# Five weight buffers with two filled early, a gather for each expert, and a later start of the first layer's modulation

## What is computed

```python
for l in range(DEPTH):                                   # first block, two layers
    proj = rms_norm(x, norm_g[l]) @ w_in[l]
    mixed = three_attentions(proj)
    x = x + mixed @ w_out[l]
mod = silu(c) @ w_ada + b_ada                            # 6 rows, and 2 for the end
x = x + gt1 * (attention(modulate(rms_norm(x), sh1, sc1)) @ w_out_2)
t = modulate(rms_norm(x, g_ffn), sh2, sc2)
g_idx = argmax(t @ w_rg + b_rg)                          # one of 4 groups
top_v, top_i = top_k(expert logits of that group, 2)     # two of its 8 experts
combine = softmax(top_v) * p_g, placed at the two experts
for e in range(32):
    a = silu(t @ w_gate[e]) * (t @ w_up[e])              # 2048 x 512, twice
    y = y + combine[:, e:e+1] * (a @ w_down[e])          # 512 x 2048
x = x + gt2 * y
return modulate(rms_norm(x, g_final), shf, scf)
```

## Time and profile before

| | |
|---|---|
| median of 3 runs | 2290.01 us (2289.23 to 2295.55) |
| the profiled execution | 2292.39 us, span of the trace 2290.6 us |
| PE busy | 2131.1 us, 93% of the span |
| PE weight loads busy | 1624.5 us, 71% |
| DVE busy | 1378.4 us, 60% |
| ACT busy | 727.2 us, 32% |
| moved by DMA | 761.71 MB, 333 GB/s over the span |

### The profile page before, as it was taken

The page is one execution under the profiler, slowest core; times in us unless marked ns, Lnnn a source line. Parts: engine busy times, 40 slices in busy tenths (PEclk is TensorE's granted clock), DMA queues, the critical chain, the costliest instruction groups (busy, mean ns, idle before and its releaser), DMA issues. The chain is left out here.

```text
span 2290.6 us, 35420 instructions
## 1 busy us (share of the span) xinstructions
PE 2131.1 (93%) x14355; PEld 1624.5 (71%) x14355; DVE 1378.4 (60%) x2159; ACT 727.2 (32%) x1317; POOL 40.8 (2%) x64
## 2 busy tenths in 40 slices
PE   7999999999999999899999979998888888888886
PEld 6799999888999998788997755554444444444443
DVE  6888899988888999755556453333333333333334
ACT  5444555454445554556555220000000000000001
POOL 0010000000000000120000000000000000000000
PEclk9999999999999999999999989999999999999998
DMA  9988777988887779654444199999999999999996
GB/s 345 353 334 320 290 276 278 356 340 344 321 324 280 282 282 373 233 213 148 138 150 163 37 385 430 430 430 430 430 430 430 430 430 430 430 430 430 430 430 282
DMA packets 72673, 761.71 MB, mean 333 GB/s; under 512 B 8256, under 2 KB 11248, under 8 KB 13936
## 3 DMA queue, kind: packets, MB, share of 16 engines
q1 hardware_dynamic: 72416, 759.37, 82.7%
q10 hardware_dynamic: 144, 0.79, 0.1%
HBM read 757.17 MB, written 2.96 MB: 332 GB/s over the span
## 5 line engine op out<-in xcount | busy, mean ns | idle before, releaser
L1218 DVE TENSOR_TENSOR s_w_tail<-s_raw,s_w_head 128x1024 fp32r<-128x1024 f32 x292 | 345.5, 1225 | 21.4 <-ACT s_w_head L827 20.9
L827 ACT ACTIVATE s_w_head<-s_raw 128x1024 fp32r<-128x1024 f32 x292 | 294.7, 1052 | 151.6 <-DMA s_raw<-in_w 97.2
L1006 PE MATMUL b_ps<-s_h_head,s_w_head 128*128 128x256 f32 x1184 | 341.8, 289 | 0.0
L1008 PE MATMUL b_ps<-s_h_head,s_w_tail 128*128 128x256 f32 x1184 | 334.8, 283 | 0.0
L1007 PE MATMUL b_ps<-s_h_tail,s_w_head 128*128 128x256 f32 x1184 | 334.8, 283 | 0.0
L1329 DVE CUSTOM_DVE_ANT_0 s_raw<-s_raw,s_c_row 128x2048 f32<-128x2048 f32 x128 | 292.5, 2285 | 3.6 <-DMA s_c_row<-c_row_dram 3.5
L2447 PE MATMUL b_ps<-s_raw,s_window 128*64 128x256 f32 x2048 | 227.6, 380 | 38.6 <-DMA s_raw<-in_w_up 20.6
L2447 PEld LDWEIGHTS b_ps<-s_raw,s_window 128*64 128x64 f32 x2048 | 155.1, 137 | 116.3 <-issue 30.6
L1006 PEld LDWEIGHTS b_ps<-s_h_head,s_w_head 128*128 128x128 f32 x1184 | 226.8, 192 | 1.9 <-issue 1.4
L1007 PEld LDWEIGHTS b_ps<-s_h_tail,s_w_head 128*128 128x128 f32 x1184 | 226.9, 192 | 0.5
L1008 PEld LDWEIGHTS b_ps<-s_h_head,s_w_tail 128*128 128x128 f32 x1184 | 226.7, 191 | 0.0
(11 more groups left out here) (361 smaller groups left out, 3395.6 us busy)
## 6 DMA issues: line engine op xcount, KB each, us to landing
s_raw<-in_w SPq DMA_DIRECT2D x198, 1024.0 KB, 5.3
s_raw<-in_w_ada SPq DMA_DIRECT2D x128, 1024.0 KB, 6.4
s_raw<-in_w_gate SPq DMA_DIRECT2D x16, 4096.0 KB, 32.8
s_raw<-in_w_up SPq DMA_DIRECT2D x16, 4096.0 KB, 30.7
s_raw<-in_w_down SPq DMA_DIRECT2D x32, 2048.0 KB, 26.9
s_down<-in_w_down SPq DMA_DIRECT2D x16, 2048.0 KB, 27.4
s_spare<-in_w_gate SPq DMA_DIRECT2D x8, 4096.0 KB, 32.9
s_down<-in_w_gate SPq DMA_DIRECT2D x8, 4096.0 KB, 32.9
```

What stands on the lines that cost most here:

```text
L827: act.activation(w_head[:, g % SPLITS, cols], raw[:, ring, cols], ACT.Copy)\
L1006: pe.matmul(out, head, m_head, start=first, stop=False, skip_group_check=True)
L1008: return pe.matmul(out, tail, m_head, start=False, stop=last, skip_group_check=True)
L1218: dve.tensor_tensor(w_tail[:, g % SPLITS, cols], raw[:, slot["w", g], cols], w_head[:, g % SPLITS, cols].bitcast(F32), ALU.subtract)\
```

## The change

There are four edits.

1. **Modulation.** In layer 0 `ada_after` now places `w_ada` pieces after weight pieces 8 to 71, one each, in place of 16 of every 18 from piece 0. Layer 1 keeps its pattern.
2. **Ring of five.** The ring has five buffers, each for a whole matrix. Two of them, `gate_slot` and `up_slot`, lie in memory that the second block has free near its end. SP loads expert 0's gate matrix in four parts between the last weight pieces of the second block, and its up matrix after the last piece. A down matrix comes as one transfer, except the last one.
3. **A gather for each expert.** `picked`, `x_head` and `x_tail` are gone, and so is the copy L2672. `picked(...)` on DVE builds a `pick` of 64 places for the next expert, with the norm's factor in it, and `gather()` on PE multiplies the plain tokens with it: 16 feature tiles, two token tiles each, stationary 128x128, 64 moving columns, fp32. This stands in each expert between the up product and the turns, for all experts but the last. ACT and DVE write the next window with gain and shift (`window_half`, 8 instructions each).
4. **Sum in a copy.** The experts' sum goes to `x_out`, a copy of x that ACT makes once, since the gather reads x to the end.

```diff
+ADA_FROM = 8
...
-def ada_after(i):
+def ada_after(l, i):
+    if l == 0:
+        return i - ADA_FROM if 0 <= i - ADA_FROM < ADA_PIECES else None
     group, k = divmod(i, 18)
     return 16 * group + k if k < 16 and 16 * group + k < ADA_PIECES else None
...
# second block, SP
             sp.dma_start(raw[:, i % RAW, :], d["w2"][i]).then_inc(sem[f"raw{i % RAW}"], 16)
+            chunk = i - (n_pieces - 7)
+            if 0 <= chunk < FT:
+                sp.wait_ge(sem["onormed"], at("onormed", "B"))
+                sp.dma_start(gate_slot[:, chunk, :],
+                             d["w_gate"][0][:, chunk * CHUNK_ELEMS:(chunk + 1) * CHUNK_ELEMS])\
+                    .then_inc(shared["arrived"][0] if chunk == FT - 1 else shared["first_gate"], 16)
...
+        sp.wait_ge(sem["tail_split"], at("tail_split", (n_pieces - 1, 1)))
+        sp.dma_start(up_slot[:, :, :].rearrange("p c n -> p (c n)"), d["w_up"][0]).then_inc(shared["arrived"][1], 16)
...
# experts, SP
-        for c in range(PIECES_E):
-            load_expert_piece(sp, 0, c)
-        sp.wait_ge(sem["picks"], 1)
+        load_matrix(sp, 0, 2)
+        sp.wait_ge(sem["sums_read"], 1)
...
+            load_matrix(sp, 1, 0, 1)
+            load_matrix(sp, 1, 1, 1)
+            sp.wait_ge(sem["used"], 1)
+            load_matrix(sp, 1, 2, 1)
...
# experts, PE
+        def gather():
+            for k in range(KT):
+                out = psum[:, 6 + k // 8, k % 8 * WINDOW:(k % 8 + 1) * WINDOW]
+                for t in range(TT):
+                    ins = pe.matmul(out, x_tiles[:, t, k, :], pick[:, t, :], start=t == 0, stop=t == 1)
+            ins.then_inc(sem["gathered"], 1)
...
+            if not last:
+                pe.wait_ge(sem["picks"], of(1, 2))
+                pe.wait_ge(sem["x_added"], of(4, 4))
+                gather()
...
+                if t and not last:
+                    pe.wait_ge(sem["window_a"], of(1, 2))
+                    pe.wait_ge(sem["window_v"], of(1, 2))
...
# experts, DVE
+        def picked(chain, places_now):
+            chain.link(dve.tensor_tensor(found[:, :, :], repeated(places_now, WINDOW), places, ALU.is_equal))
+            chain.link(dve.tensor_tensor(pick[:, :, :], found_t[:, :, 0, :], found_t[:, :, 1, :], ALU.add))
+            dve.tensor_tensor(pick[:, :, :], pick[:, :, :], repeated(rstd3[:, :], WINDOW), ALU.mult)\
+               .then_inc(sem["picks"], 1)
+        def window_half():
+            for k in range(KT // 2, KT):
+                ins = dve.tensor_scalar(window[:, k, :], psum[:, 7, (k - 8) * WINDOW:(k - 7) * WINDOW],
+                                        gain[:, k:k + 1], shift[:, k:k + 1], ALU.mult, ALU.add)
+            ins.then_inc(sem["window_v"], 1)
...
+            with dve.Fori(0, EXPERTS - 1) as e:
+                loop = Chain(dve, sem["dve_chain"], chain.n, e, 7)
+                weighed(loop)
+                dve.wait_ge(sem["weighed"], e + 1)
+                loop.link(dve.tensor_copy(current[:, :], from_start[:, bass.ds(e + 1, 1), :]
+                                          .rearrange("p a n -> p (a n)")))
+                picked(loop, current[:, :])
+                gate_times_up(loop, e)
+                dve.wait_ge(sem["gathered"], e + 2)
+                window_half()
+                add_to_x(e)
```

More of the change, by code:

```diff
@@ new lines, in _, with filled @@
+        with pe.If(few):
+            pe.wait_ge(sem["picks"], 1)
+            gather()
+            pe.wait_ge(first_gate, 16 * (FT - 1))
+            pe.wait_ge(sem["window_a"], 1)
+            pe.wait_ge(sem["window_v"], 1)
+            with pe.Fori(0, EXPERTS // RING) as five:
+                for j in range(RING):
+                    def of(each, n):
+                        return five * (RING * each) + (j * each + n)
+                    def filled(c):
+                        return five * 48 + ((3 * j + c) // RING * 16 + 16)
+                    expert(of, filled, j)
+            for e in range(EXPERTS // RING * RING, EXPERTS):
+                expert(lambda each, n: e * each + n,
+                       lambda c: 16 * ((3 * e + c) // RING + 1),
+                       e, e == EXPERTS - 1)
@@ L2659, in _ @@
-            dve.tensor_copy(weigh_w2, twice(weigh[:, :, 0:WINDOW])).then_inc(sem["picks"], 1)
-            with dve.Fori(0, EXPERTS) as e:
-                loop = Chain(dve, sem["dve_chain"], chain.n, e, 3)
+            link(dve.tensor_tensor(from_start[:, :, :], across(place_of[:, :, :].rearrange("p t n -> p (t n)"), EXPERTS),
+                                   repeated(starts[:, 0:EXPERTS], 2 * TT), ALU.subtract))
+            dve.wait_ge(sem["gathered"], 1)
+            window_half()
+            dve.wait_ge(sem["consts"], 32)
@@ new lines, in _, with weighed @@
+            dve.wait_ge(sem["x_copied"], TT)
+            dve.memset(current[:, :], 0.0).then_inc(sem["x_added"], 4)
+            dve.wait_ge(sem["x_added"], 4)
+            def weighed(chain):
+                for t in range(TT):
+                    both = weigh_w[:, t, :].rearrange("p (a s) -> p a s", a=2)
+                    ins = dve.tensor_scalar(both, across(found[:, 2 * t, :], 2), rs[:, 7, t:t + 1], None, ALU.mult)
+                chain.link(ins)
+                for t in range(TT):
+                    both = weigh_w[:, t, :].rearrange("p (a s) -> p a s", a=2)
+                    ins = dve.scalar_tensor_tensor(out=both, in0=across(found[:, 2 * t + 1, :], 2),
+                                                   scalar=rs[:, 8, t:t + 1], in1=both, op0=ALU.mult, op1=ALU.add)
+                ins.then_inc(sem["weighed"], 1)
@@ L2680, in _ @@
                        .then_inc(sem["y_scaled"], 1)
-                dve.tensor_copy(weigh_w2, twice(weigh[:, :, bass.ds(start, WINDOW)]))
                 for t in range(TT):
```

387 lines of the change are left out of this document (171 added, 216 removed).

## The result

| | median us | runs | ratio to before, 95% interval |
|---|---|---|---|
| before | 2292.4 | 4 | |
| after | 2483.8 (2479.41 to 2486.98) | 4 | 1.0833 [1.0814, 1.0853] |

The kernel became 8.3% slower. The forecast was 2451 us; the time lies 33 us above it, inside the given range (2400 to 2485) and just outside the forecast's own (2430 to 2480). The profiled execution after took 2486.98 us, span 2485.1 us, so the spans differ by 194.5 us.

What follows compares the result with a forecast made beforehand. The experts were taken as bound by weight transfers, then by PE. Modulation -9, first gather -8.8, longer experts +180.8, last expert -1.9 sum to +161.1 on 2290.0: 2451.1 us; range 2400 to 2485, forecast's own 2430 to 2480.

Steps and rivals of the forecast that it cites:

- The bound moves from DMA to PE: Experts: 29.25 us of transfers bound each before; with the gather PE needs 34.6 us, so transfers no longer bound.
- The gather's 7.2 us: Between up and turns in each expert: 64 records at 0.1125 us, paced by the weight load, 7.2 us.
- The rivals of a hidden load (3.6 to 5.2 us): Experts' gather: loads hide behind matmuls, 3.6 us at least, 5.2 by the skill's 81 ns; 2339 to 2430 us, chance 0.10.
- a falling clock inside the experts: Rival, experts' gather: half clock granted, 13.4 us a gather, 2643 us, or 2480 to 2643 if partly; chance 0.08.
- An expert of 34.6 us: Each expert on PE: 27.10 + 7.2 + 0.3 = 34.6 us against 28.77 before, 31 times, +180.8 us.
- The 0.3 us added around the gather: PE's waits on `picks`, the earlier sum and `weighed` around each expert's gather: +0.3 us (0 to 0.5).
- Ring of five ... they are worth nothing after the first expert: Fifth buffer and early loads in the experts: with PE as the bound, counted 0 (up to +2).
- The first gather: From routing to first gate product: earlier start, 9.1 us gather with half clock for 4 us; -8.8 us.
- The bound for half clock through the gather and the first gate records (-2): First gather's upper bound: clock stays at half for the whole gather and first gate records, -2 us.
- The modulation: Kernel's start, layer 0: PE's stalls and the half clock after them mostly go; -9 us, bounds -12 and +2.
- The last expert: Last expert: no gather, and its up matrix is already there; 1.85 us less.

Runs made afterwards that it cites:

- 9: On experiment 1, the first expert's gate and up matrices loaded when the experts start, not in the second block: 2440.7 us, ratio 1.0653.
- 6: On experiment 1, only 64 of 128 feature columns loaded as stationary operand in the experts' gathers: 2334.4 us, ratio 1.0188.
- 7: On experiment 1, 128 moving columns in place of 64 over the same loads in the experts' gathers: 2442.6 us, ratio 1.0665.
- experiment 1: The changed kernel with PE's loop over the experts written out, no jump back: 2441.2 us, ratio 1.0656.
- 8: On experiment 1, 11 products of 512 columns into an unused bank keep PE busy in the routing: 2433.7 us, ratio 1.0625.
- experiment 3: The kernel before with PE's loop over eight experts in place of four, body 2880 in place of 1440: 2299.4 us, ratio 1.0038.

## Right and wrong, step by step

- **The bound moves from DMA to PE: right.** DMA share 0.86, no wait on a transfer, and early loads worth nothing (9).
- **The gather's 7.2 us: right**, and the reason too (6, 7). The rivals of a hidden load (3.6 to 5.2 us) fall. So does a falling clock inside the experts: 1.00 over 800 us in experiment 1.
- **An expert of 34.6 us: 0.6 too long.** It is 33.99. The 0.3 us added around the gather has the wrong sign. With no waits on `picks` or `weighed` to be seen, what surrounds the gather shrank: from the turns to the down product 1.51 us became 1.32 (the 0.16 us for the hidden rows is gone), and the wait at the next gate product went from 0.91 to 0.72 us. Worth 31 x 0.6 = -19 us against the forecast.
- **The loop: the step that failed.** "Ring of five ... they are worth nothing after the first expert" looked at the buffers only. A ring of five makes PE's loop cover five experts, and with the gather its body grows from 1440 to 2440 matmuls and weight loads. The jump back costs a wait of 6.8 to 8.4 us in place of 0.72, and some 2 us of half clock behind it, five times: +42 us (experiment 1: 42.6). The sum had no term for it, nor had a rival. A ring of five without the gather would have a body of 1800, between 1720 and 1880; whether the ring alone brings the stall is not shown.
- **The first gather: the term was mis-sized.** -8.8 forecast, -3.9 measured, and +2.9 at the gate product behind. I let the clock recover after 4 us, as in the long gather before. These short records didn't bring it back in 13.92 us. The bound for half clock through the gather and the first gate records (-2) was the nearer one, and with -1.0 for the two together even it lay short; keeping PE busy gives 7.5 us back (8).
- **The modulation: right, a little large.** -9 forecast, -7.4 in the trace, -6.5 to -6.8 in the runs. PE has no wait left between 28 and 76 us, where the earlier trace rows had 7.8 us, and the clock from 35 to 40 us is 1.00. The 7.4 of one pair of traces holds some chance: the reduction, at 1328.40 us before, comes at 1325.4 and 1325.7 us in the traces of experiment 3 and of the modulation undone, which have the old modulation too. And the products of the router's logits (L2056) ran partly at half clock after, 3.31 us against 1.89 before (L2031) and 1.89 in experiment 1, whose code there is the same.
- **The last expert**: -1.85 forecast, -1.4 measured.

The misses add up: +1.6 (modulation), +4.9 (first gather), +2.9 (first gate product), -18.9 (expert), +42.4 (loop), +0.5 (end) = +33.4 us, the whole of 194.5 - 161.1. That the forecast missed by only 33 us owes something to the expert's overestimate, which hid nearly half of the missing term. That the median lies in the given range, 1.2 us under its upper end, is luck: the range ended at 2485 to take in a little of the falling clock, which did not come, and not for a stall of the loop.

## What to carry to other kernels

When a change unrolls a loop further or puts more into its body, count the matmuls and weight loads in PE's body: in these kernels the jump back was free at 1720, and at 1880 it cost some 7 us and a spell of half clock. Write the loop out, or keep it short; such a stall can hide under transfers and comes to light when that cover is spent. For a gather by products, count full stationary loads (0.112 us each in fp32), since up to 128 moving columns ride along free.

## What the runs showed of the hardware

- A wait "issue" of PE at a loop's head, 6.8 to 8.4 us, goes with its code being read again: the instruction queue has 126 packets where the body is 1880 and 80 where it is 1720, and 121 against 76 for eight and four experts in the loop of the kernel before. What exactly the limit counts, and why 1880 is over it, stays open.
- After a nearly idle stretch PE ran 13.92 us of back-to-back products of 64 columns at 1.2 GHz. The same products ran at 2.4 GHz when products of 512 columns stood directly before them.
- A stall of PE costs more than its length: the product behind each of the five took 8.69 to 9.89 us in place of 7.1.
